# Turning the modulation rows to columns: four transposes and a VectorE sum in place of four fp32 products with a summing matrix

## The reference: what is computed

```python
def _adaln(cvec, w, b):
    m = (jax.nn.silu(cvec) @ w + b)[:, None, :]
    return jnp.split(m, 6, axis=-1)          # w is 2048 x 12288

mod_p = _adaln(cond_ctx, w_mod[l], b_mod[l])
mod_s = _adaln(c, w_mod[l], b_mod[l])
hp = _modulate(xp, norm1_g[l], mod_p[0], mod_p[1])
...
xp = xp + mod_p[2] * out_p
```

## Time and profile before

| | |
|---|---|
| time, median of three runs | 2967.99 us (2966.01 to 2969.82) |
| time of the profiled execution | 2965.36 us |
| its span, first to last instruction | 2963.6 us |
| TensorE products busy | 2722.1 us (92%), 21024 records |
| TensorE weight loads busy | 2458.5 us (83%) |
| VectorE busy | 1522.2 us (51%) |
| ScalarE busy | 1220.6 us (41%) |
| HBM traffic | 601.38 MB read, 204 GB/s over the span |
| mean granted TensorE clock | 0.936 of full speed |

### The profile page before, as it was taken

The page is one execution under the profiler, slowest core; times in us unless marked ns, Lnnn a source line. Parts: engine busy times, 40 slices in busy tenths (PEclk is TensorE's granted clock), DMA queues, the critical chain, the costliest instruction groups (busy, mean ns, idle before and its releaser), DMA issues. The chain is left out here.

```text
span 2963.6 us, 52612 instructions
## 1 busy us (share of the span) xinstructions
PE 2722.1 (92%) x21024; PEld 2458.5 (83%) x21024; DVE 1522.2 (51%) x1800; ACT 1220.6 (41%) x1488; POOL 0.5 (0%) x6
## 2 busy tenths in 40 slices
PE   6799956979999999999979998667979999999997
PEld 1488945868888888899978896565979999999996
DVE  0533345364454454476674442433575566557666
ACT  0333312234444344355544343122345555555553
POOL 0000000000000000000000000000000000000000
PEclk9899967989999999999989997676989999999998
DMA  9678700757877777765537861021535555555552
GB/s 390 270 289 305 288 18 25 263 201 302 312 290 302 303 300 295 297 238 185 182 111 296 304 213 52 17 88 43 185 122 185 181 182 183 183 179 185 184 185 80
DMA packets 171544, 608.34 MB, mean 205 GB/s; under 512 B 18680, under 2 KB 26872, under 8 KB 171128
## 3 DMA queue, kind: packets, MB, share of 16 engines
q1 hardware_dynamic: 170872, 603.12, 56.0%
q10 hardware_dynamic: 512, 2.97, 0.3%
HBM read 601.38 MB, written 4.63 MB: 204 GB/s over the span
## 5 line engine op out<-in xcount | busy, mean ns | idle before, releaser
L438 DVE TENSOR_TENSOR w_lo<-raw,w_hi 128x1024 fp32r<-128x1024 f32 x756 | 920.8, 1225 | 1090.6 <-ACT w_hi L431 1083.0
L431 ACT ACTIVATE w_hi<-raw 128x1024 fp32r<-128x1024 f32 x756 | 796.2, 1058 | 1216.3 <-PE banks L562 627.7
L560 PE MATMUL banks<-xs_ffn,w_hi 128*128 128x256 f32 x4224 | 1204.2, 285 | 15.0 <-DVE xs_ffn L697 14.1
L561 PE MATMUL banks<-xs_ffn,w_hi 128*128 128x256 f32 x4224 | 1197.3, 283 | 0.0
L562 PE MATMUL banks<-xs_ffn,w_lo 128*128 128x256 f32 x4224 | 1196.9, 283 | 0.0
L560 PEld LDWEIGHTS banks<-xs_ffn,w_hi 128*128 128x128 f32 x4224 | 812.5, 192 | 53.7 <-issue 26.7
L561 PEld LDWEIGHTS banks<-xs_ffn,w_hi 128*128 128x128 f32 x4224 | 812.7, 192 | 0.0
L562 PEld LDWEIGHTS banks<-xs_ffn,w_lo 128*128 128x128 f32 x4224 | 812.7, 192 | 0.0
L524 PE MATMUL banks<-raw,cond 128*32 128x512 f32 x1536 | 217.1, 607 | 27.4 <-PEq L592 17.2
L560 PE MATMUL banks<-xs_odd,w_hi 128*128 128x256 f32 (+2 forms) x640 | 183.4, 286 | 7.7 <-DVE xs_odd L697 7.7
L561 PE MATMUL banks<-xs_odd,w_hi 128*128 128x256 f32 (+2 forms) x640 | 181.5, 284 | 0.0
(11 more groups left out here) (274 smaller groups left out, 2430.6 us busy)
## 6 DMA issues: line engine op xcount, KB each, us to landing
raw<-in_w_mod SPq DMA_DIRECT2D x384, 512.0 KB, 6.0
raw<-in_ffn_w_up SPq DMA_DIRECT2D x352, 512.0 KB, 5.8
raw<-in_ffn_w_down SPq DMA_DIRECT2D x176, 512.0 KB, 3.3
raw<-in_even_w_in SPq DMA_DIRECT2D x72, 512.0 KB, 8.4
raw<-in_odd_w_in SPq DMA_DIRECT2D x64, 512.0 KB, 8.4
raw<-in_even_w_out SPq DMA_DIRECT2D x32, 512.0 KB, 8.9
raw<-in_odd_w_out SPq DMA_DIRECT2D x32, 512.0 KB, 3.4
raw<-in_odd_w_tail SPq DMA_DIRECT2D x8, 448.0 KB, 3.7
```

The lines of the kernel that those rows point to most:

```text
L431: act.activation(w_hi[:, o % SPLIT], raw[:, s % RAW], ACT.Copy).then_inc(hi_done.sem, 1)
L438: dve.tensor_tensor(w_lo[:, o % SPLIT], raw[:, s % RAW], w_hi[:, o % SPLIT].bitcast(F32), ALU.subtract).then_inc(lo_done.sem, 1)
L560: pe.matmul(made, hi, x_hi, start=start and not second, stop=False, skip_group_check=second)
L561: pe.matmul(made, hi, x_lo, start=False, stop=False, skip_group_check=second)
```

## The change

The summing matrix is gone. `turn_mod` transposes the four 128 x 128 blocks of `mod_rows` into the whole of bank 6 or 7, where every group of 128 columns holds the four quarters of 32 side by side. `add_mod_bias` first sums the two used columns of each quarter over the quarters on VectorE (32 numbers in, 8 out, for each partition) into a new SBUF tile `mod_sums`, waits for that sum, and adds the bias from there. Before the sum it waits for its own previous bias addition, since `mod_sums` is a single buffer.

```diff
@@ constants()
-    for stream in range(2):
-        c[stream::QUAD, C_SUM + stream] = 1.0
@@ trunk()
+        mod_sums = sb("mod_sums", [P, GROUP, 2])
...
+        mod_summed = tally("mod_summed")
@@ turn_mod()
             for t in range(GROUP):
-                mm = pe.matmul(banks[:, MOD_COLS + j % 2, 2 * t:2 * t + 2], mod_rows[:, j % 2, P * t:P * t + P],
-                               const[:, C_SUM:C_SUM + 2], start=True, stop=True)
+                mm = pe.transpose(banks[:, MOD_COLS + j % 2, P * t:P * t + P], mod_rows[:, j % 2, P * t:P * t + P], ident)
             mm.then_inc(rows_turned.sem, 1)
@@ add_mod_bias()
-            dve.tensor_tensor(mod[:, l, tiles_at(tile, GROUP), :],
-                              banks[:, MOD_COLS + j % 2, 0:2 * GROUP].rearrange("p (t s) -> p t s", s=2),
+            quads = banks[:, MOD_COLS + j % 2, :].rearrange("p (t q s) -> p t s q", t=GROUP, q=QUADS)
+            wait(dve, mod_done.sem, f.mod_group(i, j))
+            dve.tensor_reduce(mod_sums[:], quads[:, :, 0:2], X_AXIS, ALU.add).then_inc(mod_summed.sem, 1)
+            dve.wait_ge(mod_summed.sem, f.mod_group(i, j) + 1)
+            dve.tensor_tensor(mod[:, l, tiles_at(tile, GROUP), :], mod_sums[:],
                               over(bias[:, tiles_at(tile, GROUP)], 2), ALU.add).then_inc(mod_done.sem, 1)
```

## The result

The changed kernel takes **2901.5 us** (median of four runs, 2896.68 to 2902.2) against 2967.0 us for the kernel before beside it: a ratio of 0.9775, with a 95% interval of 0.9758 to 0.9792. The sign was right and the size was not.

What follows compares the result with a forecast made beforehand. TensorE was taken to bound the four stretches holding 39 of 48 groups (busy 1054.68 of 1059.00 us). -17.5 us there plus 0.5 on VectorE made -17.0, from 2967.99 to 2951.0 us, range 2946 to 2961.

Steps and rivals of the forecast that it cites:

- The sum: Whole kernel: -17.5 us on TensorE plus 0.5 us on VectorE make -17.0 us, so 2951.0 us on the median.
- What the four products cost now: Old summing products in the FFN's loop: 1.25 us less three 0.12 us steps, so 0.89 us of TensorE a group.
- Four transposes cost 0.44 us a group: New transposes on TensorE: one pass each, four records 0.11 us apart, no seam to the next product taken.
- the rival of the seams: Drain and today's seam both paid behind every group: saving only 8.2 us, VectorE up to 1.0, 2960.8 us; chance 0.08.
- 0.45 us saved for each of 39 groups: TensorE in the four stretches where modulation runs between other products: 0.89 less 0.44 us a group, -17.5 us in all.
- The feed holds: Loads keep up with TensorE in those stretches, DMA share about 0.80; the rival, loads become the bound, 2968.5 us, chance 0.04.
- Two passes: Rival: fp32 transposes made in two passes, eight records a group as before, 0.88 for 0.89 us, 2968 us; chance 0.05.
- The clock: Rival: each group's transposes bring on 4.9 us of low TensorE clock, 64 us lost, 3032 us; chance 0.03.
- VectorE, +0.25 us at each block end: New reduction 0.2 us plus wait 0.05, paid only at two block ends: +0.5 us (0.3 to 1.0).
- Clock steps in later phases, 2 us: Later phases meet clock steps at other moments: about 2 us, taken off 2951.0 for the range's lower end.

Runs made afterwards that it cites:

- the spare tile alone: Kernel before with only an unused 32-byte SBUF tile per partition added ahead of `lam`, the four summing products kept: 2915.1 us, ratio 0.9821.
- the sum in place: Changed kernel without `mod_sums`, the quarters summed straight into `mod` and the bias added there, every buffer in its old place: 2954.24 us, ratio 0.9952.

## Why the prediction was off

**The step that failed** is "The sum". Its two terms are prices of instructions, and the step between own products, 0.12 us from rows 4 in "What the four products cost now", goes into them as a constant that is the same before and after. The diff's first added line, the tile `mod_sums`, has no term at all, and no reason is given for that. Its price, by the spare tile alone, is **-52.6 us**, three times the whole forecast: some 3 ns less for every split product, which the change was thought to leave alone. That it has the sign of the forecast is luck. What the prediction did price came out: with the buffers in their old places the new instructions take 2954.24 us, inside the range of 2946 to 2961. No row of before shows the dependence, since there all four moving operands stand at one distance. But the sum had no bound for it either, on whichever side: 18,048 products carry over 2000 us of the span, so 1 ns in the step is 18 us, and the range of 15 us held for less than that. In the kernel as it stood such a tile could hardly cost anything (the distance of 0 is one of the two worst tried), which only runs could tell.

**Point by point, the rest:**

*Four transposes cost 0.44 us a group.* The total is right, its parts are not quite. With the sum in place, where own products keep the old step, the same place reads

```profile
1099.04 0.28 PE L563 MATMUL banks<-xs_ffn,w_lo 128*128 128x256 f32 x1
1099.16 0.60 PE L538 MATMUL banks<-const,mod_rows 128*128 128x128 f32 x4
1099.52 0.36 PE L561 MATMUL banks<-xs_ffn,w_hi 128*128 128x256 f32 x1
...
1099.84 0.29 PE L563 MATMUL banks<-xs_ffn,w_lo 128*128 128x256 f32 x1
```

1099.84 - 1099.04 = 0.80, less 0.36: 0.44 again. The four last 0.60 us and one lasts 0.27, so they start 0.11 apart, the last at 1099.49; the next product follows it after 0.03 (1099.52), and a seam of 0.08 stands behind that product (0.20 to the next one). I had written 0.11 and no seam: what the seam costs, the early product gives back. That the total fits is thus luck in part, two errors of 0.08 against each other. No drain shows, and the rival of the seams is out.

*0.45 us saved for each of 39 groups.* Right. The starts with the sum in place:

```profile
L561 PE MATMUL banks<-xs_ffn,w_hi x4224: 277/283/552, 647.7 to 2928.0; 128*128 128x256 f32 x192
L561 PE MATMUL banks<-xs_odd,w_hi x640: 276/283/554, 1530.4 to 1789.1; 128*128 128x256 f32 x160
L561 PE MATMUL banks<-xs_even,w_hi x576: 277/283/553, 121.8 to 367.4; 128*128 128x256 f32 x192
L561 PE MATMUL banks<-xs_out,w_hi x512: 278/283/550, 514.8 to 2143.3; 128*128 128x256 f32 x171
```

Layer 0's FFN is 9.9 us shorter (882.7 for 892.6 between the first products of `xs_ffn` and `xs_odd`), for 22 x 0.45 = 9.9. The two input projections are 3.7 and 2.7 us shorter, the output projection 1.1. That is 17.4 us together, for a forecast of 17.5. The other stretches gave some of it back (first phase +1.3, attention +2.4, layer 1's inner work +2.7), so that -13.4 is left of the forecast -17.0 (-10.8 between the two profiled spans).

*The feed holds.* Right, and beyond what was asked of it: the DMA share went to 0.82 in the FFN's stretch (660 to 1255), and PE's list of waits is empty there.

*Two passes.* Out: 192 records for 192 tiles.

*The clock.* Out in the four stretches, where it is granted at 1.00 beside all of the transposes. The Trainium skill ("TensorE: Matmul & The Clock Gate", Part 4: PE-mode transpose) says that its full rate doesn't engage for transposes; the rows of line 539 don't agree with it, for short runs of four between products of the split operands. The prediction's own ground against this rival was rows 10, by which twenty transposes "bring the clock up". That was read from one trace, and it doesn't hold in the next: with the sum in place the same twenty, behind 4.75 us of idle PE, all run at 0.50 (median 421 ns, shortest 421, where the kernel before has 273 for the shortest), and the 32 products behind them do so too (below).

```profile
L1076 PE MATMUL banks<-const,qkv x20: 421/421/447, 413.0 to 417.1; 128*128 128x128 f32 x20
```

*VectorE, +0.25 us at each block end.* Right for the pair itself: the reduction takes 0.18 us (taken: 0.2), and the timeline at the first block's end, for rows 7, has the pair in 0.39 us, 0.23 more than the addition alone:

```profile
103.86 0.18 DVE L548 TENSOR_REDUCE mod_sums<-banks 128x8 f32<-128x32 f32 x1
104.08 0.17 DVE L550 TENSOR_TENSOR mod<-mod_sums,par 128x8 f32<-128x8 f32 x1
```

But the first phase as a whole loses more. In the six traces with the old instructions the input projection begins at 120.3 to 120.5 us, in the eleven with the new ones at 121.3 to 121.9, wherever the buffers lie. In the changed kernel the pair begins at 103.86 where the addition alone began at 103.27, so most of it stands already ahead of the pair. The prediction gave the groups of this phase neither gain nor loss; why they lose about a microsecond is open.

*Clock steps in later phases, 2 us.* Too small, and laid on the wrong side: the range has them as a gain. In the two stretches of layer 0's attention and layer 1's inner work, where the granted clock changes between its two levels, time came back. One line shows it: the 32 products of line 1291 before, and the same products (line 1292) with the sum in place (windows of PE: length, busy, records, clock, DMA share, GB/s):

```profile
420.81:424.28 3.47, 3.46 (x32) 1.00 0.61 181
```

```profile
418.48:424.96 6.48, 6.47 (x32) 0.50 0.62 205
```

In the kernel before the clock was up again by 419.00, ahead of these products; with the sum in place it is still at 0.50 all through them, which costs 3.0 us. The attention as a whole, from its first product to `xs_out`, then layer 1's inner work, before and with the sum in place:

```profile
374.00:514.80 140.80, 87.63 (x394) 67.38 (x394) 72.75 (x55) 31.96 (x38) 0.00 (x0) 0.67 0.04 12
1807.40:1940.40 133.00, 93.40 (x362) 64.32 (x362) 45.23 (x66) 26.82 (x44) 0.00 (x0) 0.62 0.05 19
```

```profile
371.60:514.70 143.10, 87.31 (x394) 66.94 (x394) 72.58 (x55) 32.07 (x38) 0.00 (x0) 0.69 0.04 12
1793.70:1929.50 135.80, 96.38 (x362) 67.01 (x363) 45.34 (x66) 26.86 (x44) 0.00 (x0) 0.60 0.05 19
```

2.3 and 2.8 us longer with the same work: 5 us, more than the gap of 3.6 between -13.4 and -17.0. That the moments of the clock's steps are what differs is shown for line 1291, whose 3.0 us are more than the whole 2.3 (the attention's mean clock alone doesn't tell it, being 0.69 for 0.67). For the second stretch it is argued from the mean clock (0.60 for 0.62) and PE's busy time (3 us more).

**The sum with the missing term.** -17.0 for the instructions, -60 for the step on 18,048 products (-58 with 3.2 ns), and +6.3 that the changed kernel gives back in the two inner stretches (3.8 and 2.5 in the table) make -69 to -71; measured are -65.5, and -63.8 between the two profiled spans, from which the table comes. By the spans 5 to 7 us are open. The table puts 2.0 of them into the output projection (-1.9 where 768 products and three turnings would give -3.9), 1.3 to 1.5 into layer 1's input projection (-7.5 for -8.8 to -9.0), 0.7 to 1.3 into layer 0's FFN (-29.5 for -30.2 to -30.8), 0.8 into the first phase, and the rest into layer 0's input projection. The stretch behind `cq` fits: 7296 products x 3.2 ns = 23.3. The cause of this rest is open.

## What to carry to other kernels

When a diff adds or resizes a buffer, list what is allocated behind it, and compare two traces first in a stretch that the change doesn't touch: if an untouched instruction has another duration there, no sum over instructions will explain the result. To learn what an edit's instructions do, run them with the buffers in their old places, and the new places with the old instructions; here two runs split the change's -65.5 us into -13.4 and -52.6. Where one kind of product fills a span, its step is worth a search of its own: a single spare tile, tried at several sizes, gave more here than the change it came with.

## What the runs showed of the hardware

- The step of a stream of split products (256 moving columns, 128 x 128 weights) depends on where the moving operand lies against the weights in a partition, modulo 256 bytes: 120.0 ns at a distance of 0, 116.6 at 32, 118.3 at 48, 117.7 at 64, 119.9 at 96, 118.6 at 128 and 160, 118.3 at 224, and 113.3 or 117.7 at 192 (all in layer 1's FFN, one execution each, two at 192). At 32, too, one execution had 117.7 there. Shown is that it is the relative place of these two operands; why a distance has its step is open. No run tells whether reads of the two meet in some part of SBUF, or whether writes of `w_hi` and `w_lo` by ScalarE and VectorE, which move with the weights, take part.
- At a distance of 192 one and the same kernel steps at either of two paces for a whole phase (2650 or 2550 products in 300 us), at a granted clock of 1.00. What picks the pace is open.
- At a clock of 1.00 a product of the split operands starts 0.03 us behind a transpose that stands ahead of it, and the product behind that 0.20 us later instead of 0.12. Four transposes in a row stand 0.11 us apart.
- Behind 4.8 us of idle PE twenty transposes run alone. In the trace of the kernel before the granted clock rises among them (0.50 up to 419.00 us, 0.98 in the 2 us behind that); with the sum in place all twenty and the 32 products behind them run at 0.50. What decides is open.
